# Equal slots for both experts of a pair, and fp32r split products for the gather and the sums

## The reference, cut to what matters

```python
p_group = softmax(xf @ wr_g + br_g); pg, gi = top_k(p_group, 1)          # one of 4 groups
pv, pi = top_k(softmax(logits of that group), 2)                        # two of its 8 experts
gates = pg * pv / sum(pv); expert_id = gi * 8 + pi
a, b = split(x_e @ w_gu[e], 2);  y_e = (silu(a) * b) @ w_down[e]        # e = 0..31, for the tokens it was given
out[token] += gate * y_e[token]
```

## Time and profile before

| | |
|---|---|
| median of three runs | 2206.72 us (2201.84 to 2209.57) |
| profiled execution, its own time | 2208.49 us |
| its span, first to last instruction | 2206.7 us |
| mean granted clock of TensorE | 0.974 |
| TensorE matmul busy | 2080.8 us, 94% of the span |
| VectorE, ScalarE busy | 884.1 us (40%), 687.7 us (31%) |
| DMA, mean over the span | 273 GB/s |
| all of L945 and L957 (the experts' products), busy | 446.1 and 226.4 us |

### The profile page before, as it was taken

One profiled execution on the slowest core, in us unless ns is written; L12 is line 12 of the kernel. 1 busy time (PEld: TensorE's weight loads), 2 busy tenths in 40 slices (PEclk: granted clock), 3 DMA queues, 4 the chain that ended last, 5 costly groups with the idle time before them and its releaser, 6 DMA issues.

```text
span 2206.7 us, 37943 instructions
## 1 busy us (share of the span) xinstructions
PE 2080.8 (94%) x15688; PEld 1519.7 (69%) x15689; DVE 884.1 (40%) x1459; ACT 687.7 (31%) x1070; POOL 80.3 (4%) x119
## 2 busy tenths in 40 slices
PE   7997899998999998889999999989998999999998
PEld 5876899988999898744544444588987444444454
DVE  5866677755643544521111111156366111111112
ACT  3434455253553456511111111144342111111111
POOL 0110111101000200000000000000000000000000
PEclk9998999999999999989999999989998999999999
DMA  9731388912654251689999999625642899999992
GB/s 360 266 128 39 118 306 320 333 42 77 249 190 175 78 189 39 255 330 422 421 422 422 421 422 422 267 90 189 214 189 98 366 421 421 422 422 422 422 422 123
DMA packets 108115, 603.25 MB, mean 273 GB/s; under 512 B 10078, under 2 KB 10532, under 8 KB 58868
## 3 DMA queue, kind: packets, MB, share of 16 engines
q1 hardware_dynamic: 95872, 559.39, 64.0%
q0 software_dynamic: 11872, 42.35, 5.2%
q10 hardware_dynamic: 276, 0.13, 0.0%
HBM read 600.74 MB, written 1.05 MB: 273 GB/s over the span
## 4 chain that ended last, share of the span: by engine, by line
PE 85%; DVE 5%; ACT 4%; DMA 3%; issue 3%; SPq 0%; DVEq 0%; ACTq 0%
PE bank L945 20%; PE bank L957 10%; PE bank L552 10%; PE bank L553 9%; PE bank L554 9%; PE bank L929 6%; PE bank L976 5%; PE bank L582 4%; DMA dense_w<-in_w_in 1%; PE bank L562 1%; PE bank L563 1%; PE bank L561 1%; PE bank L632 1%; DMA dense_w<-in_mlp_w 1%; ACT w_high L428 1%
## 5 line engine op out<-in xcount | busy, mean ns | idle before, releaser
L945 PE MATMUL bank<-expert_w,work 128*32 128x512 f32 (+1 forms) x4032 | 446.1, 593 | 19.1 <-issue 19.1
L945 PEld LDWEIGHTS bank<-expert_w,work 128*32 128x32 f32 (+1 forms) x4032 | 156.7, 110 | 307.0 <-issue 307.0
L435 DVE TENSOR_TENSOR w_low<-dense_w,w_high 128x2048 fp32r<-128x2048 f32 x112 | 256.1, 2290 | 223.5 <-ACT w_high L428 222.9
L428 ACT ACTIVATE w_high<-dense_w 128x2048 fp32r<-128x2048 f32 x120 | 228.6, 1911 | 313.4 <-DMA dense_w<-in_mlp_w 197.6
L957 PE MATMUL bank<-expert_w,work 128*32 128x512 f32 (+1 forms) x2016 | 226.4, 594 | 0.0
L2092 DVE TENSOR_TENSOR work<-work,bank 128x512 f32<-128x512 f32 x32 | 22.0, 688 | 391.4 <-ACT work L1419 391.4
L929 PEld LDWEIGHTS bank<-work 128*128 128x128 f32 x1088 | 137.3, 205 | 43.9 <-issue 43.9
L957 PEld LDWEIGHTS bank<-expert_w,work 128*32 128x32 f32 (+1 forms) x2016 | 63.6, 110 | 144.4 <-issue 144.4
L929 PE MATMUL bank<-work 128*128 128x128 f32 x1088 | 143.7, 293 | 13.9 <-issue 7.7
L552 PE MATMUL bank<-u_pairs_mlp,w_high 128*128 128x256 f32 x512 | 146.1, 285 | 7.3 <-ACT u_pairs_mlp L1144 5.9
L553 PE MATMUL bank<-u_pairs_mlp,w_low 128*128 128x256 f32 x512 | 145.6, 284 | 0.0
(11 more groups left out here) (387 smaller groups left out, 3610.3 us busy)
## 6 DMA issues: line engine op xcount, KB each, us to landing
expert_w<-in_expert_w_gu SPq DMA_DIRECT2D x256, 1024.0 KB, 13.5
expert_w<-in_expert_w_down SPq DMA_DIRECT2D x128, 1024.0 KB, 9.8
dense_w<-in_mlp_w SPq DMA_DIRECT2D x64, 1024.0 KB, 5.3
dense_w<-in_ret_w_in SPq DMA_DIRECT2D x24, 1024.0 KB, 5.3
u<-in_ada_w POOLq DMA_DIRECT2D x40, 512.0 KB, 6.0
work<-in_ada_w POOLq DMA_DIRECT2D x40, 512.0 KB, 7.0
dense_w<-in_fox_w_in SPq DMA_DIRECT2D x16, 1024.0 KB, 5.1
dense_w<-in_w_in SPq DMA_DIRECT2D x12, 1024.0 KB, 7.9
```

The source lines that it names most:

```text
L428: nc.scalar.activation(HIGH_OF[at], dense_w[:, at % RING], ACT.Copy, scale=scale).then_inc(S("w_high_ready"), 1)
L435: ins = nc.vector.tensor_tensor(w_low[:, at % RING], dense_w[:, at % RING], high, ALU.subtract)
L945: last = mm(free[half][cols, :], rows[:, k, cols], pieces[:, k // 2, a, k % 2, half * 512:(half + 1) * 512], start=k == 0, stop=k == KT - 1)
```

## The change

- Both experts of every pair have 64 slots. `UNIT`, `SHARES`, `tiles_of`, the shares' arithmetic on VectorE and two of the three copies of `project` and of `down` go. The number of further rounds is now decided by `crowd` against 64 for every pair.
- The normalised tokens are kept as two fp32r parts, `hn_high` and `hn_low`. `gather` multiplies each with the 0/1 `pick`: 32 fp32r products of 128 moving columns in place of 16 fp32 ones. The transposes ahead of them write even and odd columns apart, so that each stationary operand is a contiguous stretch.
- y is kept as `y_high` and `y_low`, already multiplied by the slot's weight (`slot_w`, a sum over the turned pick), and `pickT` is 0/1: 16 fp32r products of 256 moving columns in place of 8 fp32 ones. ScalarE makes both halves of `y_high`, VectorE both halves of `y_low` after it.
- The load of `ffn_gain` is issued behind the last of the first block's modulation weights.

```diff
-UNIT = 32
-SHARES = (UNIT, 2 * UNIT, 3 * UNIT)
...
-        hn_tok = part(wk, 0, TT, D)
+        hn_high = parts("hn_high", "work", 0, [TT, D])
+        hn_low = parts("hn_low", "u", 0, [TT, D])
...
-        y_sb = part(wk, 5632, D)
-        pick = part(wk, 6656, TT, P)
+        y_high = parts("y_high", "work", 5632, [D])
+        y_low = parts("y_low", "work", 9728, [D])
+        pick = parts("pick", "work", 6656, [TT, P])
...
-        pick_wT = part(wk, 7680, TT, P)
+        pickT = parts("pickT", "work", 7680, [TT * P])
+        slot_w = small[:, 92:93]
...
+                        last = nc.tensor.transpose(apart, h[:, k, tt * P:(tt + 1) * P], ident)
                     last.then_inc(tile_ready, 1)
                 t = TILES[f"router_{l}"]
...
                         for tt in range(TT):
-                            last = mm(free[2 + half][:, (k % 4) * P:(k % 4 + 1) * P], every_other(hn_tok[:, tt], k),
-                                      source[:, tt, :], start=tt == 0, stop=tt == TT - 1)
+                            for x in (hn_high, hn_low):
+                                last = mm(free[2 + half][:, (k % 4) * P:(k % 4 + 1) * P], x[:, tt, k * P:(k + 1) * P], source[:, tt, :],
+                                          start=tt == 0 and x is hn_high, stop=tt == TT - 1 and x is hn_low)
                     return last
 
-                def tiles_of(first):
-
-                    if first == SLOTS:
-                        return [(slice(0, SLOTS), 0), (slice(SLOTS, P), 1)]
-                    return [(slice(at, at + UNIT), int(at >= first)) for at in range(0, P, UNIT)]
-
-                def project(rows, loaded, used=None, first=SLOTS):
+                sides = [(slice(0, SLOTS), 0), (slice(SLOTS, P), 1)]
+
+                def project(rows, loaded, used=None):
 
                     for k in range(KT):
...
-                            for cols, a in tiles_of(first):
+                            for cols, a in sides:
                                 last = mm(free[half][cols, :], rows[:, k, cols], pieces[:, k // 2, a, k % 2, half * 512:(half + 1) * 512],
...
-                        last = mm(total[k // 2][:, (k % 2) * SEQ:(k % 2 + 1) * SEQ], y_sb[:, k * P:(k + 1) * P],
-                                  pick_wT.rearrange("p t n -> p (t n)"), start=False, stop=False)
+                        for y in (y_high, y_low):
+                            last = mm(total[k // 2][:, (k % 2) * SEQ:(k % 2 + 1) * SEQ], y[:, k * P:(k + 1) * P], pickT,
+                                      start=False, stop=False)
...
-                    first_rows = pe.value_load(more_i[0:1, ds(i + 2 * PAIRS, 1)], min_val=UNIT, max_val=P - UNIT)
...
-                            project(xg, loaded, expert_used, first)
+                    project(xg, loaded, expert_used)
 
                     pe.wait_ge(S("pick_ready"), count + 1)
                     pending(count)
...
                 act.wait_ge(S("hn_stats"), 2 * l + 2)
-                for q in (0, 2):
-                    t = TILES[f"hn_{l}"] + q
-                    evac(fn(hn_tok[:, 0, q // 2 * 512:(q // 2 + 1) * 512], bank(t)[:, :], ACT.Copy, scale=small[:, 88:89]), t)
-                fn(y_sb[:, 0:512], const[:, 0:512], ACT.Copy, scale=0.0).then_inc(S("y_act"), 1)
+                for q in range(4):
+                    fn(hn_part(hn_high, q), bank(TILES[f"hn_{l}"] + q)[:, :], ACT.Copy, scale=small[:, 88 + q % 2:89 + q % 2]).then_inc(S("hn_high"), 1)
+                for half in range(2):
+                    fn(y_high[:, half * 512:(half + 1) * 512], const[:, 0:512], ACT.Copy, scale=0.0).then_inc(S("y_act"), 1)
                 act.wait_ge(S("in_late"), 16 * 5)
 
...
+                    for half in range(2):
+                        fn(y_high[:, half * 512:(half + 1) * 512], free[2 + half][:, :], ACT.Copy, scale=slot_w).then_inc(done, 1)
 
...
+                    act.wait_ge(S("pick_wT_ready"), (PAIRS + 1) * l + i + 2)
...
+                link(V.tensor_scalar(steps, K("iota")[:, 1:FURTHER + 1], float(SLOTS), None, ALU.mult))
                 dve.wait_ge(S("hn_moments"), 5 * l + 4)
                 V.tensor_tensor(small[:, 84:86], small[:, 80:82], small[:, 82:84], ALU.add).then_inc(S("hn_stats"), 1)
-                V.memset(y_sb[:, 512:1024], 0.0).then_inc(S("y_dve"), 1)
-                V.memset(pick_wT, 0.0).then_inc(S("pick_wT_ready"), 1)
+                V.tensor_scalar(y_low, const[:, 0:D], 0.0, None, ALU.mult).then_inc(S("y_dve"), 1)
+                V.tensor_scalar(pickT, const[:, 0:SEQ], 0.0, None, ALU.mult).then_inc(S("pick_wT_ready"), 1)
                 dve.wait_ge(S("hn_moments"), 5 * l + 5)
                 V.reciprocal(small[:, 88:90], small[:, 86:88]).then_inc(S("hn_stats"), 1)
                 dve.wait_ge(S("hn_stats"), 2 * l + 2)
-                for q in (1, 3):
-                    t = TILES[f"hn_{l}"] + q
-                    evac(V.tensor_scalar(hn_tok[:, 1, q // 2 * 512:(q // 2 + 1) * 512], bank(t)[:, :], small[:, 89:90], None, ALU.mult), t)
+
+                def low_of_hn(q):
+                    dve.wait_ge(S("hn_high"), 4 * l + q + 1)
+                    evac(V.scalar_tensor_tensor(hn_part(hn_low, q), bank(TILES[f"hn_{l}"] + q)[:, :], small[:, 88 + q % 2:89 + q % 2],
+                                                hn_part(hn_high.bitcast(f32), q), ALU.mult, ALU.subtract), TILES[f"hn_{l}"] + q)
+                low_of_hn(0)
+                low_of_hn(1)
                 iota = K("iota")
                 bias = rowbc[:, ROW_ROUTER + NR * l:ROW_ROUTER + NR * (l + 1)]
                 t = TILES[f"router_{l}"]
...
                 t = TILES[f"router_{l}"] + 1
                 wait_tile(dve, t)
...
-                V.tensor_tensor(by_choice[1], pick_e[:, 0:2, :, :], both(room[:, 0:1, :].broadcast_to([P, TT, E])), ALU.mult)
-                link(V.tensor_tensor(key_first, pos, room[:, 1:2, :].broadcast_to([P, TT, E]), ALU.add))
-                V.tensor_tensor(by_choice[2], pick_e[:, 0:2, :, :], both(key_first), ALU.mult)
-                link(V.tensor_reduce(held, by_choice[1], AX.X, ALU.add))
-                V.tensor_reduce(rel[:, :, :], by_choice[2], AX.X, ALU.add)
-                for n in range(1, FURTHER + 1):
-                    last = V.scalar_tensor_tensor(gone[:, :, n - 1], rt[:, 30:34], float(n), rt[:, 26:30], ALU.mult, ALU.is_le)
-                link(last)
+                place = rt[:, 26:30].rearrange("p (c t) -> p c t", c=2)
+                chosen = number.rearrange("p t c -> p c t")
+                pos = bank(t)[:, 0:TT * E].rearrange("p (t n) -> p t n", t=TT)
+                counts = bank(t)[:, 2 * E:3 * E].rearrange("p (i a) -> p a i", a=2)
+                crowd, more, upto = (share[:, b, :] for b in range(3))
+                link(V.tensor_tensor(by_choice, pick_e[:, 0:2, :, :], pos.unsqueeze(1).broadcast_to([P, 2, TT, E]), ALU.mult))
+                V.tensor_copy(crowd, counts[:, 0, :])
+                link(V.tensor_reduce(place, by_choice, AX.X, ALU.add))
+                evac(V.tensor_tensor(crowd, crowd, counts[:, 1, :], ALU.max), t)
+                V.scalar_tensor_tensor(rel[:, :, :], chosen, float(SLOTS), place, ALU.mult, ALU.add)
+                link(V.tensor_tensor(gone, rt[:, 26:30].unsqueeze(2).broadcast_to([P, 2 * TT, FURTHER]),
+                                     steps.unsqueeze(1).broadcast_to([P, 2 * TT, FURTHER]), ALU.is_ge))
                 link(V.tensor_reduce(rounds.rearrange("p c t -> p (c t)"), gone, AX.X, ALU.add))
-                link(V.scalar_tensor_tensor(rel_more[:, :, :], held, -float(ROUND_KEY), rounds, ALU.add, ALU.mult))
-                link(V.tensor_tensor(rel[:, :, :], rel[:, :, :], rel_more[:, :, :], ALU.subtract))
+                link(V.scalar_tensor_tensor(rel[:, :, :], rounds, float(ROUND_KEY - SLOTS), rel[:, :, :], ALU.mult, ALU.add))
 
                 def build_pick(keys, plain, weighted, linked, plain_done, weighted_done):
 
...
                     V.tensor_tensor(rows[:, 4:8, :], free[3][:, :].rearrange("p (k n) -> p k n", k=4), gains, ALU.mult).then_inc(done, 1)
 
                 def take_pick_wT(done):
-                    V.tensor_copy(pick_wT, free[1][:, 0:SEQ].rearrange("p (t n) -> p t n", t=TT)).then_inc(done, 1)
-
-                def take_y(done):
-                    V.tensor_copy(y_sb[:, 512:1024], free[3][:, :]).then_inc(done, 1)
+                    V.tensor_reduce(slot_w, free[1][:, 0:SEQ], AX.X, ALU.add)
+                    V.tensor_scalar(pickT, free[1][:, 0:SEQ], 0.0, None, ALU.is_gt).then_inc(done, 1)
+
+                def take_y(made, at, done):
+                    for half in range(2):
+                        dve.wait_ge(made, at + half + 1)
+                        eight = slice(half * 512, (half + 1) * 512)
+                        last = V.scalar_tensor_tensor(y_low[:, eight], free[2 + half][:, :], slot_w, y_high[:, eight].bitcast(f32),
+                                                      ALU.mult, ALU.subtract)
```

(7 more changed lines are left out.)

75 lines of the change are left out of this document (20 added, 55 removed).

## The result

The kernel after takes 2280.2 us, the median of four runs (2274.45 to 2285.32), the kernel before 2208.1, again of four. The ratio is 1.0312, with a 95% interval of 1.0274 to 1.0349: **slower, by some 70 us**. The prediction was 2260 us, within 2232 to 2312. The profiled execution took 2274.45 us, its span is 2272.7; against the 2206.7 us of before that is +66.0, where the prediction's sum had +53. (It was the fastest of the four, so the medians lie 6 us further apart than the two profiles.)

The account below looks back on a forecast made before the run. TensorE sets the pass at 29.57 us, with the DMA already slightly slower at 29.84, hidden by the weights' lead. +75 (first layer) - 17.8 (second) - 3 - 1 (edges) = +53 us on 2206.7: 2260 us, range 2232 to 2312.

Parts of the forecast that it names:

- An ordinary pass, 27.4 us: TensorE's steady pass over an expert pair: 13.87 + 3.87 + 0.69 + 1.93 + 7.02 us, in place of 29.57.
- `gather` in fp32r at the price of its weight load: Each of 32 narrow fp32r products in `gather` takes 0.12 us, a full weight load: 3.87 us, no change.
- rival of 7.74 us a pass: Narrow fp32r products in `gather` cost as much as fp32 ones, a pass 31.3 us, whole kernel 2371 us; chance 11%.
- rival of 1.93 us: `gather` takes 1.93 us through faster weight loads, 1.94 us off each pass and round; 2237 us, chance 5%.
- its own rival of faster loads: Faster fp32r weight loads in `gather`: second layer -20, first +54, whole kernel 2237 us; chance 5%.
- Second layer, -17.8 us: Second expert loop: 460.2 us against 478.0, TensorE waiting for weights after six or seven passes, the DMA setting the layer.
- Three further rounds, on the pairs 8, 10 and 11: First layer: experts with 68, 78 and 77 choices do not fit 64 slots, so three rounds come that the shares avoided.
- A round of 36.5 us: One further round in the first layer, from the end of the pair's `down` through branches, nothing overlapping; bounds 30 and 45.
- First layer, +75 us: First expert loop: 16 x 27.4 + 2.7 + 3 x 36.5, and 3 for first-run code: 553 us against 478.0.
- Edges, -3 and -1 us: Before the loops 1.5 us gained for each layer by VectorE's shorter chain; behind the loops nothing, to 0.5 us.
- `ffn_gain`, 0: The moved 8 KB load costs 0; in the wrong place no more than the 6.2 us it takes to land.
- No further rounds, 2167: Rival: routing leaves each expert at 64 or less, both layers gain, 40 us less, 2167 us; chance 4%.

Follow-up runs that it names:

- e9_half_columns: The kernel after with half of every weight piece's columns loaded for the second layer's pairs 1 to 15, on all 128 rows; 2253.0 us in one run, second loop 434.5.
- e3_slots_only: The kernel after, its 64 slots kept, with gather and sums in fp32 as in before; 2277.9 us, 1.0303 of before.
- e1_no_rounds: The kernel after with the threshold for a further round set out of reach, so no pair gets one; 2172.3 us, 0.9829 of before.
- e4_one_turn: The kernel after with its loop over further rounds making one turn instead of three on every engine; 2270.0 us, 1.0273 of before.
- e11_double_rounds: The kernel after with a second, empty further round in each of the three crowded pairs; 2395.9 us in one run, first loop 680.4.
- e12_gain_moved: The kernel before with only the load of `ffn_gain` put behind POOL's loads for the MLP's modulation; 2208.9 us, ratio 1.0002.
- e10_sum_only: The kernel after with only the gather back in fp32, the sums left as split products; 2273.9 us, 1.0273 of before.
- e5_half_weights: The kernel after with 64 of 128 partition rows of each weight piece loaded for the second layer's pairs 1 to 15; second loop 474.4 us, passes 30.7.
- e2_shares_split: The shares of the kernel before, with gather and sums as split products as in after; 2207.6 us, 1.0001 of before.
- e8_straight: The kernel after with shares of 32 and 96 only for pairs with one expert over 64, rare code behind one test; 2194.0 us, 0.9935 of before.

## Why the prediction was right, and where it was off

The verdict, the mechanism and the order of the terms were right. It missed the median by 20 us: 13 in the sum (+53 for +66), the rest between the medians and what the profiles show. The sizes follow by its own steps.

- **An ordinary pass, 27.4 us.** Measured 27.15. `gather` 3.63 for 3.87 (a step is 0.11, not 0.12 us), `add_up` 2.08 for 1.93, `down` 6.92 for 7.02.
- **`gather` in fp32r at the price of its weight load.** Right. The rival of 7.74 us a pass and the rival of 1.93 us both fell. The load takes 192 ns for 128 columns, 188 in the first MLP, and half as many moving columns shorten the step only from 0.12 to 0.11 us. The 81 ns of the Trainium skill (TensorE: Matmul & The Clock Gate, Back-to-back issue gap) are not reached: the trace has 110. The prediction put them at some 24 us; counted like its own rival of faster loads, where the weights hold the second layer and the first up to pair 8, the same 1.27 us in 8 passes and 3 rounds, with 2 us in the second layer, make an estimate of 16.
- **Second layer, -17.8 us.** Measured -16.0, and `e9_half_columns` shows that it is the transfers' time that sets it. The turn came with the sixth pass, the first longer than 27.15 us. What I had not asked is which part of the change this gain belongs to. By `e3_slots_only` it is the variants: without them fp32 products would have done nearly as well.
- **Three further rounds, on the pairs 8, 10 and 11.** Right, and `e1_no_rounds` shows that they decide the sign.
- **A round of 36.5 us.** This is the mis-sized term. The three take 42.0, 39.4 and 39.4 us, 40.3 on average, and 1.75 us more in the `project` behind each: 126 us where I had 109.5 and 3 for first code. In the round that begins at 1270.0 each step runs a little late: the gather ends 0.8 us later, by VectorE's later `pick_more`, and `down` ends at 34.9 for 33.9. The tail is the larger part: 4.5 us from `down` to the next `project` where I had 2.6. That is 3.0 for y and two empty turns of 0.75 each (`e4_one_turn`, `e11_double_rounds`). The fall of the clock I had only in the upper bound; it came each time, behind the tail, and the 3 us for first code no run shows: the idle times of the first round are those of the other two, and the loop's first pass lost only the 1.75 us of a low clock. (The first round, at 42.0 us, had its own `project` at the low clock too.) At 34.8 us with the clock held, 37.4 on average (`e11_double_rounds`), a round without the way in and out is near the number predicted. (In the prediction's own range a round of 30 us makes -19.5 us, not -21.)
- **First layer, +75 us.** Measured +90.4: 16 x 27.15 = 434.4, the rounds 120.8, the slow `project` behind each and in the first pass 7.0, and 6.1 us of waits for weights ahead of pair 8 where I had 2.7. Together 568.3. The shorter pass hid 4 us of what the rounds cost more.
- **Edges, -3 and -1 us.** The ways into the loops gained more, 3.1 and 2.8 us. `e3_slots_only` gained 4.8 between the loops, which I put down to the shares' arithmetic; the split's extra copies cost some 1 to 2 (kernels with after's code there take 269.4 to 271.1 us, `e3_slots_only` 268.6). Behind the second loop 0.8 us were lost.
- **`ffn_gain`, 0.** Right as far as the runs can tell, within 0.2% (`e12_gain_moved`).
- **No further rounds, 2167.** The rival fell, but its price was good: `e1_no_rounds` took 2172.3 us.

+90.4 - 16.0 - 3.1 - 2.8 + 0.8 - 3.4 ahead of the norm at 528 us, which the prediction has no step for, makes the 66 us. The signs that I had named came: 1184 records of `gather`, 592 of `add_up`, 35 projections, and the second layer's period that turns from 27.15 to 29.83 us. The three long passes took 67 to 72 us, not 64.

## What to carry to other kernels

A fixed capacity is paid for by the data that break it: three of 64 expert loads over 64 turned a gain of 34 us into a loss of 70, so count the overflows of the real input before the common pass is made cheaper, and give the rare case its own path ahead of a straight common one. Where transfers of 29.83 us stand behind a pass of 29.57, work taken out of the pass counts only until the weights' lead is used up, and then no more: 1.5 us less in each of 16 passes shortened the second loop by 2.3 us (`e3_slots_only`, `e10_sum_only`). A stall in the first pass of such a loop is not made up, since the one buffer stops the transfers too.

## What the runs showed of the hardware

- Weight transfers of 512 KB to 64 partition rows kept the DMA engines' share at 1.01 with 203 GB/s (`e5_half_weights`); those of 512 KB to 128 rows moved at a share of 0.65 and landed, by their issues' medians, in 4.4 to 4.6 us (`e9_half_columns`). Half the bytes saved no time on half the rows, and did on all rows. The Trainium skill (Advanced Engine Details and Errata, DMA Bandwidth Details) gives the memory 16 ports of 27.2 GB/s, each for 8 partitions; an estimate by it is 8 x 27.2 = 218 GB/s for 64 rows and 435 for all. The runs have 203 and, with whole pieces, 422, and agree within 7%.
- Inside the expert loops TensorE's granted clock fell for a few microseconds to its 1.2 GHz level behind 3.7 to 4.7 us of idleness each time, and behind 2.97 us once in three (`e4_one_turn`), as behind 3.05 to 3.08 us in `e3_slots_only`. The length alone doesn't decide: it held once behind 3.34 us (`e11_double_rounds`), and the first `project` of after was slow behind 2.35 us (946.98, 15.65 us), with other waits ahead of it.
- A turn of a loop whose body is jumped over cost TensorE 0.75 us, the jump past two variants in a loop's first pass 3.7 to 4.2 us (before, `e2_shares_split`), the way into a loop past the rare code 4.6 to 4.7 us (`e8_straight`), and the first return from a rarely run block 12.88 us. No run here shows what sets these times.
